# Turning the residual rows before the norm's factor is known, and adding the weighted sums to them in the bank by matmuls

## The reference, cut to what matters

```
o = concatenate([tok, mo]) @ w_o[i]
x = x + rms_norm(o, g_mix_post[i])           # joint "ffn", i        (i = 0, 1)
h = rms_norm(x, g_ffn_pre[i])
f = (silu(gu[:, :D_FF]) * gu[:, D_FF:]) @ w_down[i]        # gu = h @ w_gate_up[i]
x = x + rms_norm(f, g_ffn_post[i])           # joint "mix", 1 (i = 0); joint "ffn1", 0 (i = 1)
```

## Time and profile before

| | us |
|---|---|
| median of three executions | 1633.84 |
| the profiled execution | 1633.79 |
| its span, first to last instruction | 1632.0 |
| PE busy | 1607.4 (98%) |
| DVE busy | 1068.5 (65%) |
| ACT busy | 882.2 (54%) |
| POOL busy | 85.4 (5%) |

### The profile page before, as it was taken

One profiled execution on the slowest core, in us unless ns is written; L12 is line 12 of the kernel. 1 busy time (PEld: TensorE's weight loads), 2 busy tenths in 40 slices (PEclk: granted clock), 3 DMA queues, 4 the chain that ended last, 5 costly groups with the idle time before them and its releaser, 6 DMA issues.

```text
span 1632.0 us, 23915 instructions
## 1 busy us (share of the span) xinstructions
PE 1607.4 (98%) x9386; PEld 1360.8 (83%) x9386; DVE 1068.5 (65%) x1323; ACT 882.2 (54%) x1306; POOL 85.4 (5%) x160
## 2 busy tenths in 40 slices
PE   9999999999999999999999999999999999999998
PEld 8768888876888888888987788888888888788887
DVE  6766666786765676656758566666666666766665
ACT  6755444675544555444557454445444556654444
POOL 1000000030000030000002000002000001000000
PEclk9999999999999999999999999999999999999999
DMA  8326555524555557555430355557655542055552
GB/s 281 130 78 200 191 184 192 186 81 140 181 183 203 180 180 248 180 199 185 157 130 2 129 190 185 192 183 224 203 183 190 177 155 79 3 185 198 184 190 92
DMA packets 197098, 270.62 MB, mean 166 GB/s; under 512 B 4856, under 2 KB 165232, under 8 KB 197024
## 3 DMA queue, kind: packets, MB, share of 16 engines
q1 hardware_dynamic: 194016, 262.08, 48.1%
q0 software_dynamic: 2544, 7.09, 1.7%
q10 hardware_dynamic: 464, 0.44, 0.1%
HBM read 268.53 MB, written 1.05 MB: 165 GB/s over the span
## 4 chain that ended last, share of the span: by engine, by line
PE 88%; DVE 7%; ACT 3%; POOL 1%; issue 1%; DMA 0%; POOLq 0%; SPq 0%; DVEq 0%; ACTq 0%
PE pair L1996 29%; PE pair L2001 15%; PE bank L1907 10%; PE bank L1908 10%; PE bank L1909 10%; PE bank L1976 4%; DVE xt L1198 1%; PE pair L1907 1%; PE pair L1909 1%; PE pair L1908 1%; POOL blk L640 1%; PE bank L2181 1%; PE pair L2130 1%; PE bank L2151 1%; DVE probs L1355 1%
## 5 line engine op out<-in xcount | busy, mean ns | idle before, releaser
L1178 DVE TENSOR_TENSOR w_lo<-raw,w_hi 128x2048 fp32r<-128x2048 f32 (+1 forms) x246 | 560.7, 2281 | 139.5 <-ACT w_hi L761 137.8
L761 ACT ACTIVATE w_hi<-raw 128x2048 fp32r<-128x2048 f32 (+1 forms) x247 | 470.4, 1908 | 272.9 <-PE pair L2001 194.8
L1996 PE MATMUL pair<-xt,w_hi 128*128 128x512 f32 x2112 | 508.9, 392 | 1.3 <-DVE xt L1198 0.2
L1996 PEld LDWEIGHTS pair<-xt,w_hi 128*128 128x128 f32 x2112 | 390.4, 188 | 87.3 <-DVE xt L1198 8.4
L2001 PEld LDWEIGHTS pair<-xt,w_lo 128*128 128x128 f32 x2112 | 270.8, 191 | 10.3
L2001 PE MATMUL pair<-xt,w_lo 128*128 128x256 f32 x2112 | 274.0, 283 | 0.0
L1907 PE MATMUL bank<-w_hi,hid_hi 128*128 128x512 f32 x528 | 206.2, 390 | 0.0
L1908 PE MATMUL bank<-w_hi,hid_lo 128*128 128x512 f32 x528 | 206.1, 390 | 0.0
L1909 PE MATMUL bank<-w_lo,hid_hi 128*128 128x512 f32 x528 | 205.4, 389 | 0.0
L1238 DVE TENSOR_TENSOR gate_sum<-pair,gate_sum 128x512 f32<-128x512 f32 x66 | 45.6, 691 | 201.1 <-ACT gate_sum L861 201.1
L1909 PEld LDWEIGHTS bank<-w_lo,hid_hi 128*128 128x128 f32 x528 | 99.2, 188 | 21.1
(11 more groups left out here) (294 smaller groups left out, 1739.0 us busy)
## 6 DMA issues: line engine op xcount, KB each, us to landing
raw<-in_w_gate_up SPq DMA_DIRECT2D x44, 1024.0 KB, 5.1
raw<-in_ffn_wg SPq DMA_DIRECT2D x44, 1024.0 KB, 5.2
raw<-in_ffn_wu SPq DMA_DIRECT2D x44, 1024.0 KB, 5.2
raw<-in_ffn_wd SPq DMA_DIRECT2D x44, 1024.0 KB, 5.0
raw<-in_w_in SPq DMA_DIRECT2D x26, 1024.0 KB, 5.1
raw<-in_w_down SPq DMA_DIRECT2D x22, 1024.0 KB, 5.0
raw<-in_w_o SPq DMA_DIRECT2D x8, 1024.0 KB, 5.1
raw<-in_w_out SPq DMA_DIRECT2D x8, 1024.0 KB, 5.0
```

What stands on the lines that cost most here:

```text
L761: act.activation(w_hi[s][:, 0:filled(u)], raw[s][:, 0:filled(u)], ACT.Copy).then_inc(hi_ready, 1)
L1178: dve.tensor_tensor(w_lo[s][:, 0:filled(u)], raw[s][:, 0:filled(u)], w_hi[s][:, 0:filled(u)].bitcast(F32), ALU.subtract)\
L1996: pe.matmul(out[:, 512 * m:512 * (m + 1)], w[0][:, c, P * m:P * (m + 1)], xt[:, 2 * SEQ * c:2 * SEQ * (c + 1)], start=(c == 0), stop=False)
```

## The change

At the joints ("ffn", 0), ("ffn", 1) and ("ffn1", 0) PE no longer waits for the summed rows. turn_sums first turns the old x: 16 products with x as the stationary and the identity as the moving operand, plain matmuls instead of transposes, which open the accumulation in the banks. Then, for each t, 8 products with osm as the stationary operand and a diagonal of the norm's factors (sum_diag, made by DVE in diagonal()) as the moving one add the weighted sums to the same banks. DVE's add_norm stands behind turn_lo, for both t, since x itself is still needed later; ACT's squares_of waits for its last piece. At ("ffn", l) the four keep_busy products between the tiles go; at ("ffn1", 0) the five and seven become four ahead of the second t. At ("ffn1", 0) the second tile's first half is scaled as soon as its squares are there. Joint ("mix", 1) stays as it was.

```
+        sum_diag = [junk[:, 768 + P * t:768 + P * (t + 1)] for t in range(NT)]
 # ACT
                 turn_hi(("ffn", l), 3 + 4 * l)
+                act.wait_ge(prep_ready.sem, prep_ready.at(("rows", ("ffn", l), 3, 1)))
                 squares_of(x, 3 + 4 * l)
...
                 turn_hi(("ffn1", l), 9 + 3 * l)
+                if l == 0:
+                    act.wait_ge(prep_ready.sem, prep_ready.at(("rows", ("ffn1", 0), 3, 1)))
                 squares_of(x, 9 + 3 * l)
 # DVE
+            def diagonal(j, name, t):
+                prep_ready.mark(("sums", name, t), 0)
+                n = norm_column(j)
+                dve.wait_ge(rstd_ready.sem, rstd_ready.at(("norm", j, t)))
+                link(dve.tensor_scalar(sum_diag[t], ident, rstd[:, n + t:n + t + 1], None, ALU.mult),
+                     prep_ready, ("sum diagonal", name, t))
...
+                prep_ready.mark(("first sums", l), 0)
                 for t in range(NT):
                     dve.wait_ge(squares.sem, squares.at(("piece", l, t, 1)))
                     sum_squares(2, 2 + 4 * l, t)
                     out_scaled(t, 1)
+                    diagonal(2 + 4 * l, ("ffn", l), t)
+                turn_lo(("ffn", l), 3 + 4 * l)
+                for t in range(NT):
                     add_norm(2 + 4 * l, ("ffn", l), t)
-                turn_lo(("ffn", l), 3 + 4 * l)
                 split_lo(u + 3 + AHEAD)
...   # second joint of layer 1; layer 0 keeps its order
+                    diagonal(8, following, 0)
+                    dve.wait_ge(squares.sem, squares.at(("half", 1, 1, 0)))
+                    scaled(1, 0)
+                    dve.wait_ge(squares.sem, squares.at(("half", 1, 1, 1)))
+                    sum_squares(2, 8, 1)
+                    scaled(1, 1)
+                    diagonal(8, following, 1)
...
                 turn_lo(("ffn1", l), 9 + 3 * l)
                 if l == 0:
+                    for t in range(NT):
+                        add_norm(8, ("ffn1", 0), t)
                     split_lo(u + 1)
 # PE
+            def turn_sums(name, fill):
+                for t in range(NT):
+                    for c in range(KC):
+                        pe.matmul(TURN[c // 2][:, SEQ * (c % 2) + P * t:SEQ * (c % 2) + P * (t + 1)],
+                                  x[:, t, P * c:P * (c + 1)], ident, start=(t == 0 and c % 2 == 0), stop=False)
+                for t in range(NT):
+                    pe.wait_ge(prep_ready.sem, prep_ready.at(("sums", name, t)))
+                    if t and fill:
+                        keep_busy(fill, ACC[0][:, 0:P])
+                    pe.wait_ge(prep_ready.sem, prep_ready.at(("sum diagonal", name, t)))
+                    for c in range(KC):
+                        last = pe.matmul(TURN[c // 2][:, SEQ * (c % 2) + P * t:SEQ * (c % 2) + P * (t + 1)],
+                                         osm[:, t, P * c:P * (c + 1)], sum_diag[t], start=False,
+                                         stop=(t == 1 and c % 2 == 1))
+                        if t and c % 2:
+                            last.then_inc(turned.sem, turned.mark((name, c // 2)))
...
-                turn_halves(("ffn", l), None, ((ACC[3][:, 0:P], 0), (ACC[3][:, 0:P], 4)))
+                pe.wait_ge(prep_ready.sem, prep_ready.at(("first sums", l)))
+                turn_sums(("ffn", l), 0)
                 keep_busy(3, ACC[3][:, 0:P])
...
-                    turn_halves(("ffn1", l), None, ((TURN[3][:, P:2 * P], 5), (TURN[3][:, P:2 * P], 7)))
+                    pe.wait_ge(gate_summed, 2 * NG)
+                    pe.wait_ge(up_summed, 2 * NG)
+                    turn_sums(("ffn1", l), 4)
                     keep_busy(3, ACC[3][:, 0:P])
```

More of the change, by code:

```diff
@@ L1596, in _ @@
                 scaled(0, 1)
[L1597 to L1602, removed]
+                if l == 0:
+                    add_norm(4, following, 0)
+                    dve.wait_ge(squares.sem, squares.at(("half", 0, 1, 1)))
+                    sum_squares(2, 4, 1)
+                    scaled(1, 0)
+                    scaled(1, 1)
+                    add_norm(4, following, 1)
+                else:
+                    diagonal(8, following, 0)
+                    dve.wait_ge(squares.sem, squares.at(("half", 1, 1, 0)))
+                    scaled(1, 0)
+                    dve.wait_ge(squares.sem, squares.at(("half", 1, 1, 1)))
+                    sum_squares(2, 8, 1)
+                    scaled(1, 1)
+                    diagonal(8, following, 1)
             def add_ffn(f, following):
@@ L1882, in turn_piece, with turn_halves @@
                 last.then_inc(turned.sem, turned.mark((name, p)))
-            def turn_halves(name, freed=None, fill=None):
+            def turn_sums(name, fill):
                 for t in range(NT):
-                    if fill:
-                        out, count = fill[t]
-                        keep_busy(count, out)
+                    for c in range(KC):
[12 more added lines that the diff above has]
+                            last.then_inc(turned.sem, turned.mark((name, c // 2)))
+            def turn_halves(name, freed=None):
+                for t in range(NT):
                     for p in range(4):
```

## The result

The changed kernel takes 1642.21 us (median of five executions, 1642.19 to 1642.5), the kernel before 1634.02 measured beside it (five executions). The ratio is 1.0052, 95% interval 1.0041 to 1.0063: slower by 8.2 us. The forecast was 1645.4 with a range of 1640.8 to 1649.2. The span grew from 1632.0 to 1640.4, by 8.4 us.

What follows compares the result with a forecast made beforehand. PE, holding 88% of the chain, was taken to lose time only where it waits. PE's products, 7.87 us, plus late sums, 3.7, made 11.6 us over 1633.79, giving 1645.4, range 1640.8 to 1649.2.

Steps and rivals of the forecast that it cites:

- A plain float32 product costs 0.224 us: On PE at each joint: each of the 32 new products takes two records 0.112 us apart, 0.224 us.
- the prediction's four passes: On PE: true FP32 takes four passes through the array, estimated at 0.213 us a product of 128 columns.
- PE at the joints, 2.79, 2.79 and 2.29: PE's new products delay ACT's first copy by 2.79 us at both ("ffn", l), 2.29 at ("ffn1", 0).
- A: Start of ACT's first copy at a joint; 116.48, 405.04 and 595.42 in the kernel before.
- Eight additions put ACT's squares 4.5 us later: Behind turn_lo on DVE: eight additions, 3.3 us, make ACT's squares start 4.5 us later, at A + 7.4.
- So everything behind them moves 4.5 us, add_cross to A+15.4, PE stands 1.2 us: Behind ACT's squares: add_cross(0) ends at A + 15.4, so PE's gate of group 1 waits 1.2 us a joint.
- The second term: PE's wait for add_cross(0) at the gate of group 1: 1.2 us at three joints, 3.7 us.
- the first term: PE's new products ahead of ACT's first copy at the three joints: 7.87 us together.
- the rival of PE's products alone: Behind turn_lo: cover takes up the additions, add_cross isn't late, only PE's products cost time; 1641.6, chance 10%.
- What is late next: U_B, met with 0.5 to spare: Addition in U_B ends at A + 20.8; PE wants U_B at A + 21.3, so 0.5 us to spare.
- the 5.5 of the rival: Clock drop in the 1.2 us wait: a 5.5 us wide product at half clock each joint, 16.5 us; 1661.9, chance 2%.
- The bound of some tenths a joint: At ("ffn", l), even with cheap products, the second tile's factor bounds the gain to some tenths a joint.

Runs made afterwards that it cites:

- the two runs on it: Kernel before, split_lo(u0 + 1) put behind the next norm's diagonals: 1634.29 us; changed kernel, two more additions behind the eight at two joints: 1643.17 us.

## Why the prediction was right, and where it was off

- *A plain float32 product costs 0.224 us.* Right: 3.57 us for 16 (0.223 each), and the run with transposing products took away the half of three times that, 5.3 us. The six records for three products are two a product, so by their number they don't bear out the prediction's four passes; what comes near its estimate of 0.213 is the time.
- *PE at the joints, 2.79, 2.79 and 2.29.* Right: A moved by 2.70, 2.72 and 2.19 behind the last product, 7.6 for 7.9. Without the turn all but 1.0 us of the loss is gone.
- *Eight additions put ACT's squares 4.5 us later.* Right: A+7.38 instead of A+2.87.
- *So everything behind them moves 4.5 us, add_cross to A+15.4, PE stands 1.2 us.* Here the sum was off: 3.7 us were forecast and 1.0 measured. add_cross ended at A+14.65, gate 1 came 0.39 to 0.44 later than before, and 0.29 to 0.34 of it lasted to up 1. The mis-sized term is POOL's step: the forecast carried the chain from the squares to the factor over as one length from the kernel before, with a step of 1.01 us in it that there waited for DVE's subtraction. In the changed kernel the subtraction starts with ACT's squares (126.34 and 126.46) and is over before they are (128.62 and 128.79), so the step takes 0.19. Three times 0.82 is 2.5 of the 3.2 us between the sum of 11.6 and the 8.4 by which the span grew; the rest are tenths, 0.3 of them at A. That the subtraction holds the step is shown in both directions by the two runs on it.
- *The range and the rivals.* The second term was nearly four times too large. That the measured time still fell in the range is owed to the first term, two thirds of the sum, and to a range wide enough to take in the rival of PE's products alone. 1642.21 lies 0.6 from that rival (1641.6, chance 10%) and 3.2 from the forecast (64%). Its condition, that what follows the additions comes 1.2 us earlier than placed, held in part: add_cross ended 0.75 earlier.
- *What is late next: U_B, met with 0.5 to spare.* The spare was right, though both times were not: U_B's addition ended at A+19.79 instead of A+20.8, up 1 started at A+20.38 instead of A+21.3, 0.59 behind it. Both hang on the chain with POOL's step in it, so both came about 1 us earlier. The spare holds for DVE's order as it stands; with add_cross moved ahead of split_lo(u0 + 2) the addition came 0.2 late.
- *The clock.* The granted clock of the changed kernel is 0.999 over the span, and its waits for add_cross stay under 0.5 us. What a wait of 1.2 us would do was not tried. After waits of 2.5 us one fall in three came, and cost 1.6 us, not the 5.5 of the rival.
- *What the change could win.* The bound of some tenths a joint held. With PE free in time, one diagonal and two products took 0.14 us longer than one addition and two transposes at ("ffn", 0) (3.67 against 3.53 us from the last product to A). The best that any run showed is 0.48 at A of ("ffn1", 0), of which 0.16 was left at up 1, and no run was faster than the kernel before.

## What to carry to other kernels

Before work is moved into an engine's wait, count its records at that engine's pace: 5.4 us in which PE did little that counts were too short for 32 plain float32 products of two records each (32 x 0.223 = 7.1 us), and the chain that was shortened was no longer the one that ended last. When a chain is carried over from a trace to a new order, take apart every duration in it that is longer than the same instruction elsewhere; it may be a wait for a neighbour that won't be there. A reordering that removes a wait of PE wins only what the next wait leaves of it: 0.06 us here, where the freed wait was 0.36.

## What the runs showed of the hardware that I had not expected

- A POOL instruction of 0.19 us took 0.83 to 1.09 us while a 2.28 us DVE subtraction ran, and 0.48 under an addition of 0.48, and ended within 0.06 us of it. Under a DVE product with one operand in a PSUM bank it took 0.19. POOL's row shows the held time as busy time, not as a wait.
- Float32 products in the transposing mode can open an accumulation to which plain float32 products then add, one record (0.109 us a product in a stream) instead of two (0.223), with a weight load for each record in both.
- After PE stood 2.5 us the clock fell to 0.50 at one of three joints and stayed at 1.00 at the other two, with the same instructions of PE before and behind.
